# Four post-norm boundaries worked by token halves and twelve pieces instead of eight whole tiles

## What is computed

```python
def rmsnorm(x, g):
    xf = x.astype(jnp.float32)
    y = xf * lax.rsqrt(jnp.mean(xf * xf, axis=-1, keepdims=True) + EPS)
    return (y * g.astype(jnp.float32)).astype(x.dtype)
...
    for l in range(DEPTH):
        u = rmsnorm(x, pre_mix_g[l])
        m = token_mixer(u, ...)
        x = x + rmsnorm(m, post_mix_g[l])
        h = rmsnorm(x, pre_ffn_g[l]) @ w_ffn_up[l]
        f = jnp.square(jax.nn.relu(h)) @ w_ffn_down[l]
        x = x + rmsnorm(f, post_ffn_g[l])
    return x
```

## Time and profile before

| | us |
|---|---|
| median of 3 runs | 2967.21 |
| lowest and highest run | 2965.1 and 2967.24 |
| span of the profiled execution | 2967.4 |

### The profile page before, as it was taken

How to read it: one execution, slowest core, us unless ns; L and a number is a source line. 1 busy time by engine, 2 the same in 40 slices (tenths; PEclk the granted TensorE clock), 3 DMA queues, 4 the chain that set the end, 5 groups by cost and what they waited for, 6 DMA issues and landing times.

```text
span 2967.4 us, 33768 instructions
## 1 busy us (share of the span) xinstructions
PE 2819.7 (95%) x12862; PEld 2308.3 (78%) x12862; DVE 1613.9 (54%) x2076; ACT 1158.8 (39%) x1785; POOL 743.7 (25%) x612
## 2 busy tenths in 40 slices
PE   8898999999998989999999878999999999999997
PEld 6676887888776778778887777788887789778886
DVE  5786446334367864465443796455534458555533
ACT  5575334222255753342222454322332348422221
POOL 2563113313125631132131161022200013122200
PEclk9999999999999999999999899999999989999999
DMA  4011322232220112223332202223232210132332
GB/s 137 29 43 36 100 92 85 95 98 99 93 78 29 43 37 99 93 85 101 99 99 93 80 23 66 93 93 100 97 103 98 86 43 1 57 99 93 99 106 86
DMA packets 75122, 236.42 MB, mean 80 GB/s; under 512 B 9776, under 2 KB 17728, under 8 KB 74976
## 3 DMA queue, kind: packets, MB, share of 16 engines
q1 hardware_dynamic: 73776, 231.05, 24.0%
q0 software_dynamic: 928, 3.27, 0.3%
q10 hardware_dynamic: 272, 0.06, 0.0%
HBM read 228.31 MB, written 2.10 MB: 78 GB/s over the span
## 4 chain that ended last, share of the span: by engine, by line
PE 85%; DVE 8%; ACT 3%; issue 1%; POOL 1%; DMA 1%; SPq 0%; DVEq 0%; POOLq 0%; ACTq 0%
PE bank L1873 27%; PE bank L1875 26%; PE bank L1874 26%; PE bank L2179 2%; PE bank L2040 1%; DVE S5S L1735 1%; DMA RAWW<-weights 1%; DVE STAT L1563 1%; DVE WL L1452 1%; ACT WH L1127 1%; DVE S5S L1726 1%; DVE PHL L1457 0%; PE bank L1982 0%; DVE CF L1513 0%; PE bank L2086 0%
## 5 line engine op out<-in xcount | busy, mean ns | idle before, releaser
L1452 DVE TENSOR_TENSOR WL<-RAWW,WH 128x1024 fp32r<-128x1024 f32 (+2 forms) x424 | 573.7, 1357 | 854.6 <-ACT WH L1127 854.4
L1873 PE MATMUL bank<-UH,WH 128*128 128x512 f32 (+1 forms) x1920 | 763.4, 398 | 55.8 <-DVE UL L1462 30.0
L1874 PE MATMUL bank<-UL,WH 128*128 128x512 f32 (+1 forms) x1920 | 755.4, 393 | 0.0
L1875 PE MATMUL bank<-UH,WL 128*128 128x512 f32 (+1 forms) x1920 | 755.2, 393 | 0.0
L1127 ACT ACTIVATE WH<-RAWW 128x1024 fp32r<-128x1024 f32 (+2 forms) x424 | 433.8, 1027 | 384.6 <-DMA RAWW<-weights 384.1
L1873 PEld LDWEIGHTS bank<-UH,WH 128*128 128x128 f32 (+1 forms) x1920 | 365.2, 190 | 145.4 <-issue 60.7
L1874 PEld LDWEIGHTS bank<-UL,WH 128*128 128x128 f32 (+1 forms) x1920 | 365.3, 190 | 78.4 <-issue 2.4
L1875 PEld LDWEIGHTS bank<-UH,WL 128*128 128x128 f32 (+1 forms) x1920 | 364.7, 190 | 77.4
L1874 PE MATMUL bank<-HL,WH 128*128 128x512 f32 x512 | 199.3, 389 | 0.0
L1873 PE MATMUL bank<-HH,WH 128*128 128x512 f32 x512 | 199.3, 389 | 0.0
L1875 PE MATMUL bank<-HH,WL 128*128 128x512 f32 x512 | 199.3, 389 | 0.0
(11 more groups left out here) (345 smaller groups left out, 4700.4 us busy)
## 6 DMA issues: line engine op xcount, KB each, us to landing
RAWW<-weights SPq DMA_DIRECT2D x424, 512.0 KB, 3.4
X<-x SPq DMA_DIRECT2D x8, 256.0 KB, 5.8
FF<-tables POOLq DMA_DIRECT2D x2, 1024.0 KB, 7.5
U<-S5U SPq DMA_DIRECT2D x32, 64.0 KB, 2.0
out<-FF SPq DMA_DIRECT2D x8, 256.0 KB, 2.0
GEL<-U SPq DMA_DIRECT2D x112, 16.0 KB, 1.8
S5B<-s_b POOLq DMA_DIRECT2D x1, 512.0 KB, 4.4
S5C<-s_c POOLq DMA_DIRECT2D x1, 512.0 KB, 3.8
```

Of the source, the lines that this page charges most:

```text
L1452: dve.tensor_tensor(slot_words(WL, c % SLOTS, size), slot_words(RAWW, c % SLOTS, size), f32(slot_words(WH, c % SLOTS, size)), ALU.subtract ...
L1873: nc.tensor.matmul(out_, w[0], x_[0], start=start, stop=False, **how)
L1874: nc.tensor.matmul(out_, w[0], x_[1], start=False, stop=False, **how)
L1875: return nc.tensor.matmul(out_, w[1], x_[0], start=False, stop=stop, **how)
```

## The change

The last two output tiles before a boundary become one step, a `pair`. Its products are made for 256 tokens at a time: front half of both tiles, then back half of both, in the banks 0, 1, 2 and 7. With two chunks for each tile (FFN) the chunks come in the order first chunk of both, second chunk of both. The four quarters are evacuated and squared one by one (`tail`), and the sums over partitions and the factor are made for each half of the tokens (`pair_total`, `post_stat`).

Scaling, add, UH, square and UL go in 12 pieces: the front halves of tiles 0 to 3, the whole tiles 4 to 7, the back halves of tiles 0 to 3. VectorE's order in a step is: UL of the piece before, add of this piece, scaling of the next. The scaling of piece 4 waits for the factor of the back half. TensorE (`piece_jobs`) runs pieces 0 to 3 for two of the lead jobs, with the back half's sum over partitions behind piece 0, then waits for the third lead chunk, catches up its pieces 0 to 3, and does the rest for all three.

The cuts of chunks N and N+1 stand among the quarters; that of N+2 now stands behind piece 5, that of N+3 behind piece 9 and thus ahead of the last pieces. Behind a mixer the jobs may use six banks in turn instead of four. The cut of the fourth chunk at the start of the program is written out ahead of the first layer.

```diff
+AHEAD = LEAD + 1
...
+NORM_BANKS = (4, 5, 0, 1, 2, 7)
+PAIR_BANKS = (0, 1, 2, 7)
+FRONT, BACK, WHOLE = slice(0, SEQ // 2), slice(SEQ // 2, SEQ), slice(0, SEQ)
+EARLY = 4
+PIECES = ([(k, FRONT) for k in range(EARLY)] + [(k, WHOLE) for k in range(EARLY, DT)]
+          + [(k, BACK) for k in range(EARLY)])
+PN = len(PIECES)
...
+        if pieces:
+            ring = (AHEAD, AHEAD, 3, 4, 5)[x] if x < min(pieces, 5) else pieces
+        else:
+            ring = LEAD + 1 if after.get("ring") or norm and x >= 2 else 2
...
+        if pieces:
+            mm[x].bank = NORM_BANKS[x % pieces]
...
+    for x in range(len(mm), singles + 1):
+        if x < singles:
             product(x)
             plan.cut_to(done_of(mm[x]) + 1)
-        elif ahead:
...
+        elif ahead == "res":
+            plan.cut_to(plan.total["c"] + LEAD - 1)
+        elif pair:
+            last = pair_of_jobs(plan, jobs[x], after)
...
+    if pair:
+        c = plan.total["c"]
+        plan.cut_to(c)
+        last.a = plan.add("tail", "a", i=0, m=singles, half=0, pair=last).a
+        plan.cut_to(c + 1)
+        plan.add("tail", i=1, m=singles + 1, half=0, pair=last)
+        plan.add("tail", "a", i=2, m=singles, half=1, pair=last)
+        return last
...
+    n = len(job["kt"])
+    pair = plan.add("pair", f"c:{2 * n} j:2 ph:2 tl:2 s:2", n=n, rhs=job["rhs"], add=after["add"], group=after["group"])
+    plan.cut_to(pair.c + n)
+    return pair
...
+    def post_norm(pair, gain, norm=None):
+        post = plan.add("post", POST, gain=gain, norm=norm, pair=pair)
+        c = plan.total["c"]
+        plan.add("post_stat", half=0, post=post)
+        for i in range(PN + 1):
+            plan.add("post_piece", i=i, post=post)
+            if i == 1:
+                plan.add("tail", i=3, m=DT - 1, half=1, pair=pair)
+            elif i == 3:
+                plan.add("post_stat", half=1, post=post)
+            elif i == 5:
+                plan.cut_to(c + LEAD - 1)
+            elif i == 9:
+                plan.cut_to(c + AHEAD - 1)
+        return post
...
+    norm = plan.add("norm", PIECE_NORM, gain=16, version=1, pieces=6)
...
+    plan.layers_post = post_norm(pair, 24)
...
+                k, cols = PIECES[i]
+                act.wait_ge(x_done.sem, x_done.room(l, PN * norm.version + i))
+                act.activation(UH[:, k, cols], X[:, k, cols], ACT.Copy, scale=gain[:, k:k + 1]).then_inc(uh.sem, 1)
+                act.activation(FF[:, k, cols], X[:, k, cols], ACT.Square).then_inc(squared.sem, 1)
...
+                elif kind == "tail":
+                    cols = (FRONT, BACK)[st.half]
+                    if st.half:
+                        act.wait_ge(bank_free.sem, bank_free.after(l, st.pair.j + st.i - 2))
                     else:
-                        square(l, st.s, FF[:, st.m, :])
-                elif kind == "post":
-                    factor(l, st.g, st.last_s, RCQ[:], 1.0 / DM, EPS)
...
+                        act.wait_ge(front_free.sem, front_free.after(l, st.pair.tl + st.i))
+                    if st.m == DT - 2:
+                        square_for_pool(l, st.pair.a + st.half, FF[:, st.m, cols], cols)
+                    else:
+                        square(l, st.pair.s + st.half, FF[:, st.m, cols], cols)
+                elif kind == "post_stat":
+                    cols = (FRONT, BACK)[st.half]
+                    factor(l, st.post.g + st.half, st.post.pair.s + st.half, RCQ[:, cols], 1.0 / DM, EPS, cols=cols)
+                elif kind == "post_piece" and st.i < PN:
+                    to, norm, gain = next_norm(l, st.post)
+                    norm_piece(to, norm, st.i, gain)
...
+            def piece_rest(l, n, i, gain):
+                k, cols = PIECES[i]
+                dve.wait_ge(uh.sem, uh.after(l, n + i))
+                dve.scalar_tensor_tensor(UL[:, k, cols], X[:, k, cols], gain[:, k:k + 1], f32(UH[:, k, cols]),
                                          ALU.mult, ALU.subtract).then_inc(ul.sem, 1)
+            def piece_scaled(l, post, i):
+                k, cols = PIECES[i]
+                if i == EARLY:
+                    dve.wait_ge(rstd.sem, rstd.after(l, post.g + 1))
+                dve.tensor_tensor(FF[:, k, cols], FF[:, k, cols], RCQ[:, cols], ALU.mult).then_inc(scaled.sem, 1)
+            def piece_added(l, post, i):
+                k, cols = PIECES[i]
+                dve.wait_ge(scaled.sem, scaled.after(l, post.sc + i))
+                dve.scalar_tensor_tensor(X[:, k, cols], FF[:, k, cols], LP[:, l, post.gain + k:post.gain + k + 1], X[:, k, cols],
+                                         ALU.mult, ALU.add).then_inc(x_done.sem, 1)
...
+                elif kind == "tail":
+                    cols, pair = (FRONT, BACK)[st.half], st.pair
+                    if st.half:
+                        dve.wait_ge(used.sem, used.after(l, pair.c + 2 * pair.n - 4 + st.i))
+                        freed = bank_free
+                    else:
+                        dve.wait_ge(front_done.sem, front_done.after(l, pair.ph + st.i))
+                        freed = front_free
+                    b = BANK[PAIR_BANKS[st.i]]
+                    if pair.add:
+                        dve.tensor_tensor(FF[:, st.m, cols], b[:, cols], FF[:, st.m, cols], ALU.add).then_inc(freed.sem, 1)
+                    else:
+                        dve.tensor_copy(FF[:, st.m, cols], b[:, cols]).then_inc(freed.sem, 1)
                 elif kind == "post":
                     dve.wait_ge(rstd.sem, rstd.after(l, st.g))
-                    to, norm, gain = next_norm(l, st)
-                    for k in range(DT + 2):
-                        if k < DT:
-                            dve.tensor_tensor(FF[:, k, :], FF[:, k, :], RCQ[:], ALU.mult).then_inc(scaled.sem, 1)
-                        if 1 <= k <= DT:
-                            t = k - 1
-                            dve.wait_ge(scaled.sem, scaled.after(l, st.sc + t))
-                            dve.scalar_tensor_tensor(X[:, t, :], FF[:, t, :], LP[:, l, st.gain + t:st.gain + t + 1], X[:, t, :],
-                                                     ALU.mult, ALU.add).then_inc(x_done.sem, 1)
-                        if k >= 2:
-                            tile_rest(to, norm.n, k - 2, gain)
+                    piece_scaled(l, st, 0)
+                elif kind == "post_piece":
...
+                    if st.i:
+                        piece_rest(to, norm.n, st.i - 1, gain)
+                    if st.i < PN:
+                        piece_added(l, st.post, st.i)
+                    if st.i + 1 < PN:
+                        piece_scaled(l, st.post, st.i + 1)
...
+            def bank_open(l, st):
+                freed = bank_free.room(l, st.j) - (st.ring - 2)
+                if freed > 0:
+                    pe.wait_ge(bank_free.sem, freed)
...
+            def piece_jobs(l, jobs, ready, pair_layer, pair):
+                xh, xl = inputs["u"]
+                for st in jobs[:2]:
+                    bank_open(l, st)
+                    pe.wait_ge(lo.sem, lo.after(l, st.c))
+                for i in range(EARLY):
+                    pe.wait_ge(*ready(i))
+                    for st in jobs[:2]:
+                        lead_product(l, st, PIECES[i][0], i, PIECES[i][1], xh, xl)
+                    if i == 0:
+                        pair_total(pair_layer, pair, 1)
+                bank_open(l, jobs[2])
+                pe.wait_ge(lo.sem, lo.after(l, jobs[2].c))
+                for i in range(EARLY):
+                    lead_product(l, jobs[2], PIECES[i][0], i, PIECES[i][1], xh, xl)
+                for i in range(EARLY, PN):
+                    pe.wait_ge(*ready(i))
+                    for st in jobs:
+                        lead_product(l, st, PIECES[i][0], i, PIECES[i][1], xh, xl)
+            def pair_total(l, st, half):
+                cols, g = (FRONT, BACK)[half], st.group + half
+                pe.wait_ge(logged.sem, logged.after(l, g - 2))
+                pe.wait_ge(added.sem, added.after(l, st.a + half))
+                nc.tensor.matmul(stat_bank(g)[:, cols], ONES, SQUARES[:, cols], start=True, stop=False)
+                pe.wait_ge(sq.sem, sq.after(l, st.s + half))
+                nc.tensor.matmul(stat_bank(g)[:, cols], ONES, TMP[:, (st.s + half) % 2, cols], start=False, stop=True
+                                 ).then_inc(summed.sem, 1)
...
+                def products(job, i, half):
+                    c = st.c + 2 * i + job
+                    cols = (FRONT, BACK)[half]
+                    pe.wait_ge(lo.sem, lo.after(l, c))
+                    for k in range(DT):
+                        w_ = slice(k * P, (k + 1) * P)
+                        ins = product(BANK[PAIR_BANKS[2 * half + job]][:, cols], (WH[:, c % SLOTS, w_], WL[:, c % SLOTS, w_]),
+                                      (xh[:, i * DT + k, cols], xl[:, i * DT + k, cols]), i == 0 and k == 0,
+                                      i == st.n - 1 and k == DT - 1)
```

(20 more changed lines are left out.)

144 lines of the change are left out of this document (81 added, 63 removed).

## The result

The changed kernel takes 2988.18 us (median of 4 runs, 2986.61 to 2989.39), the one before 2967.22 (2965.1 to 2967.24): ratio 1.0071, 95% interval 1.0059 to 1.0083, so 21.0 us slower. The profiled execution took 2989.39 with a span of 2987.6 us and a mean granted clock of 0.975 (before 0.976).

A forecast was written before the change was run, and what follows sets the result against it. TensorE was taken to bound the kernel, with VectorE's tree finishing within 0.2 us of it. Statistic times at four boundaries sum to 192.4, less 173.1 before: 19.4 us longer, 2967.2 + 19.4 = 2986.6, range 2967 to 3001.

The forecast's parts named there:

- The hole: TensorE's 8.2 us gap before the first product on the next input, predicted down to 0.5 after the mixer.
- T: Time in us at a boundary, counted from the first product of the last two output tiles.
- The back factor: Back half's factor at 17.3, after ScalarE's piece 3 work; scaling 4 waits, adding 1.8 us to VectorE's chain.
- The third chunk: Weight cut after piece 5: VectorE idles 1.8 us for ScalarE, TensorE waits 5.7 us, until 25.1.
- half clock for free: Half clock after TensorE's waits costs up to 2.9 us, inside the 3.1 left, so not counted in the sum.
- The tree: VectorE's tree of squares after the mixer: runs from 38.0 to 42.3, statistic at T = 42.5.
- the product of 256 columns: Taken as 0.117 us, so halving costs 0.3 us in a mixer pair and 0.7 in an FFN pair.
- around two cuts: 5.2 us of VectorE's longer chain at two weight cuts, where before one with 1.9 stood behind the last rest.
- Rival B: About the same: cuts cost nothing in VectorE's chain (ScalarE ahead, third chunk cut early), 2966 us; chance 0.1.
- Rival A: Faster: without waits in VectorE's chain the halves pay, tree ends at 33.9, 14 us shorter, 2953; chance 0.08.
- the 8.4 us of waits: VectorE's predicted waits per boundary: back factor 1.8, two cuts 3.5, the rest cycle latency.
- Rival C: Slower still: 256-column products at 0.15, 3003 us; or half clock behind the statistic, up to 2.9 each; chance 0.14.

The follow-up runs named there:

- the filled run of the change: The changed kernel with 16 and 38 products of 256 columns that nobody reads in TensorE's waits for UL and for the weight cut: 2992.24 us.
- the first experiment: The changed kernel with the cut of the third lead chunk moved from behind piece 5 to behind piece 1: 2991.61 us, ratio 1.0086.
- the reordered kernel: The changed kernel with the rest two pieces behind the add and the third and fourth chunks' weight cuts both behind piece 3: 2973.94 us, ratio 1.0025.
- the filled run: The reordered kernel with 33 products of 256 columns that nobody reads in TensorE's wait of 4.21 us at each boundary: 2966.17 us, ratio 0.9995.
- the kernel before, filled: The kernel before with 22 products of 512 columns that nobody reads ahead of the lead jobs at each of four boundaries: 2960.3 us, ratio 0.9979.

## Why the prediction was right

The forecast was 2986.6, the sum +19.4; measured are +21.0 by the medians and +20.4 at the four boundaries. That the range of 34 us held says little, and that the medians come within 2 us is in part luck, since the stages outside the boundaries differ by more than that between runs. What bears the prediction out is the schedule. Step by step, at the first boundary:

- **The hole.** First scaling at T = 10.6 (10.3), UL of piece 0 from 12.1 (11.8), product at 12.76 (12.6). Each is the few tenths late that the pair is, below.
- **The back factor.** Scaling 4 at 17.5 (17.3). TensorE waits from 16.6 to 18.7 (16.2 to 18.6).
- **The third chunk.** Its cut stands 1.65 for ScalarE (1.8) and starts at 23.7 (23.6); TensorE goes on at 25.1 (25.1). But its wait is 4.79 and not 5.7, since it begins later: the six products of piece 3 ahead of it ran at half clock (457.61 to 459.26). At the mixer of layer 1 they run at full clock, and the wait there is 5.46. The sum had taken half clock for free, and it was: the half clock behind both waits took 1.3 us (the filled run of the change) out of the 3.1 that the prediction saw left.
- **The tree** begins at 38.2 (38.0) and the statistic comes at 42.59 (42.5). The last rest starts 27.2 us after the first scaling (27).

The mis-sized term is the product of 256 columns: in the pair its starts are 0.12 apart, not 0.117. A pair is thus longer by 48 x (0.24 - 0.227) = 0.6 us after the mixer and 1.25 after the FFN, where I had 0.3 and 0.7. That is the 0.3 by which T after the FFN (53.99) is above 53.7. By the Trainium skill's rule on the weight load ("TensorE: Matmul & The Clock Gate", The mechanism, and LDWEIGHTS), as the prediction read it, it would have been 0.21 each; the trace disagrees.

**Two readings of the kernel before were too smooth.** VectorE does not run without a pause from 454.57: it stands 0.72 ahead of its cut, as a later sentence of the prediction has it. And "within 0.2 us of each other" holds at the first boundary alone; at the others TensorE was 0.6 to 1.6 us behind the tree. The sum took T before from the trace at each boundary, so it did not suffer.

**The attribution was less good than the sum.** I wrote 5.2 us "around two cuts". The waits of VectorE at the cuts are real (1.65 and 1.50), but the first experiment shows that an earlier cut pays the same wait; a cut was free, but for 0.25, where VectorE waits anyway, as in the reordered kernel. Rival B had this wrong: "cut early" was not enough, and the cuts in the free place, with the rest two pieces behind as well, still left 2974 to 2967. The cuts alone in that place were not run.

**Rival A** did not come about: of the 8.4 us of waits 7.1 appeared at the first boundary (all the waits in brackets of VectorE's timeline there). Its price, 14 us to the good without them, stays untested, since no run took them all out. The reordered kernel comes nearest. It still stands 1.60, 0.25 and 0.18, and its tree ends at T = 36.8; less these waits it would be about 34.7 (an estimate), where A had 33.9. TensorE did not follow even that far: at half clock it ended at 38.0, a bound that A did not count; at full clock (the filled run) it ended with the tree. The best that halves reached is 2.5 us a kernel at the boundaries (the filled run), equal by the median, and the kernel before, filled, reached 3.3.

**Rival C**'s second mechanism, half clock behind the statistic, exists. It came behind waits of 2.94 and 2.95 us ahead of the statistic; behind the change's 1.65 and 1.81 after its mixers it did not appear. Where it did, the next FFN took 1.5 to 2.9 us longer.

## What to carry to other kernels

Cutting work in halves so that the next stage can begin sooner pays only if the engine that ends the stage also ends sooner: work out its queue operation by operation, since a dependence between neighbours in that queue costs the other engine's latency at every piece. When a wait of TensorE goes, ask who is second: here VectorE's tree and TensorE's own products were within 0.2 us of each other at the first boundary before the change, and within 1.6 at the others. Work that waits for another engine is best put where its own engine waits anyway: moving two weight cuts there brought the end of VectorE's chain forward by 3.0 us a boundary, moving one early brought nothing. An idle TensorE cost twice here, once as the wait and once as the half clock behind it; the second part can be had back with products nobody reads, as long as TensorE is what ends the stage.

## What the runs showed of the hardware

- VectorE's three-operand add from SBUF took 1.76 us instead of 0.74 while a GpSimd add of 1.32 us ran, and at 256 columns 0.96 beside a GpSimd add of 0.73 and 1.51 beside one of 1.33, instead of 0.48. This I had not expected at this size. The Trainium skill ("Advanced Engine Details and Errata", GPSIMD Details) says that the Pool engine shares a read and a write interface with VectorE and conflicts with instructions with two SBUF inputs; the rows agree.
- Products of 256 columns with a weight load each start 0.12 apart at full clock and 0.21 at half clock, those of 512 columns 0.227 and 0.43.
- The granted clock followed what TensorE did before, useful or not: 19 products at half clock behind a wait of 4.21 us, none when it was filled but for 0.26.
- A wait of TensorE was not followed by the same loss each time: behind 2.94 to 2.95 us ahead of the statistic, the next FFN took 1.5, 2.9, 1.5 and 1.6 us longer.
